# Setup and retention of an encoder trunk in one block: what is loaded, summed and turned first

## The chip, the cores and the metric

The kernel runs on one core of a Trainium2 chip. The metric is the device time of one execution, in microseconds. The core has five engines with queues of their own: TensorE (PE, with its weight loads as PEld), VectorE (DVE), ScalarE (ACT), GpSimd (POOL) and SyncE (SP), which here issues nearly all DMAs. They wait for each other by semaphores.

## The reference, cut to what matters

A trunk of two layers over 2048 tokens of width 1024. Each layer modulates its normalised input by a shift and a scale that a matrix product of `silu(c)` gives; the first layer then projects it for a retention and an attention part.

```
cos, sin = _rope_tables(positions)
c_act = silu(c)
mod = c_act @ ada_w[layer] + ada_b[layer]
shift, scale, gate = split(mod, (1024, 1024, 1024))
h = rmsnorm(x, pre_g[layer]) * (1 + scale) + shift
z = h @ w_in                      # even layer: rq, rk, rv, rg, ... are columns of z
rq, rk = rope(rq), rope(rk) * 64 ** -0.5
lg = log_sigmoid(dec)             # decay of each of 4 heads, two directions
o = retention forward + retention backward, chunks of 128 tokens
```

The change touches only the beginning: the loads, the modulation sums, the rotary angles, the decays, and the first of 16 tiles of the retention's projection.

## The kernel before, in words

The kernel is a sequence of blocks. Within a block each engine runs its own program; at the end of a block all engines meet and the block's semaphores are cleared. The first block is `setup`, the second `project_retention`; attention, the odd layer and the output follow and are not touched.

`setup` loads five small tensors (`cols`, `const`, `table`, `dec_row`, `pos_i`), two tiles of x (`xt`), eight blocks `ada` of 128 rows of the modulation matrix (128x2048, 1 MB each) and the retention's weights `w_raw` in three column groups of four pieces (512 KB each), all from SP's queue in the order of `L227` to `L246`. All engines that need a small load wait for all five (`small_in` at 80).

* VectorE computes `lg`, the log of a sigmoid, with some 25 operations on 128x8 elements, each waiting for the one before (`L354` to `L370`), then the angles' whole turns (`L388` to `L390`), the exponents (`L375` to `L377`), and then the modulation: two of the eight blocks go to TensorE as matrix-vector products (`mod_ps`, `L327`), six are multiplied by `silu_c` and added up in PSUM by VectorE (`acc_ps`, `L395`, `L398`). The last sum goes to SBUF (`mod_sums`), TensorE transposes it in 16 pieces (`L332`), VectorE reduces these four at a time (`L414`) and makes `shift` and `gain` (`L417` to `L421`).
* GpSimd reduces the angles (`ang`, `bit`, `red`, `L289` to `L309`): turns times a constant, subtracted, three times over, then clipped. ScalarE takes sine and cosine (`L273`).
* A weight is kept as two float32r parts, high and low: ScalarE rounds `w_raw` to `w_hi`, and VectorE or GpSimd subtracts, `w_lo = w_raw - w_hi`. The first column group is split in `setup` (`L271`, `L406`, `L311`), the others at the start of the next block (`split_w`, `L585`, `L640`, `L691`), two pieces of each group on GpSimd and two on VectorE.

`project_retention` runs over 16 tiles of 128 tokens, the last first. For a tile, TensorE transposes the scaled x (`ps_h`), ScalarE applies `gain` and `shift` (`ht`), h is split into `h_hi` and `h_lo`, and each of three projections (`ps_qk`, `ps_v`, `ps_g`) is 24 products, three for each of eight 128-row pieces. VectorE multiplies `ps_qk` by cosine and sine (`rc`, `rs`), GpSimd adds and weights them (`qk`, `qf`, `kw`, `L627` to `L633`), TensorE transposes them and forms the state's product (`ps_kv`, `L798`). For the first tile the halves of h go to ScalarE and VectorE (`L588`, `L695`), and TensorE waits for all four `w_lo` pieces of a group before `ps_v` and before `ps_g`. The second tile begins with its first `ps_qk` product (`L761`).

Of the kernel before, what the change touches and what calls it, by code (L numbers as in the profile page):

```python
# [19 lines left out]
P = 128  # L20
D = 1024
# [136 lines left out]
def setup(nc, st, const, cols, row, positions, turning, ada_w, layer, w, w_hi, w_lo, w_raw, w_in, xt, x_pieces, xn, ps_h, spare):  # L158


    with ExitStack() as ctx:
# [3 lines left out]
        sem = counters(nc, ctx)  # L165

        NW, NPE = 6, 2
        dec_row = sb("dec_row", [1, 2 * H])
        pos_i = sb("pos_i", [P, NT], I32)
        pos = sb("pos", [P, NT])  # L170
        ang, turns_i, turns, red, bit = turning
        low = sb("low", [P, 2 * H])
        mods = sb("mods", [P, 2 * KD])
        logit = sb("logit", [P, 2 * H])
        lg = st.lg
        tiny = sb("tiny", [P, 8, 2 * H])
        expw = sb("expw", [P, 2 * H])
        expq = sb("expq", [P, H, 2])
        expk = sb("expk", [P, H, 2])
        ada = sb("ada", [P, NW, 2 * D])  # L180
        acc = spare[:]
        scale1 = sb("scale1", [P, KD])
        mods_pe = sb("mods_pe", [P, 2 * KD])
        sq = xn[:]
        ssq, ms, rstd = [[sb(f"{n}_x{i}", [P, 1]) for i in range(2)] for n in ("ssq", "ms", "rstd")]
        dec_ps = ctx.enter_context(nc.psum_tensor("dec_ps", [P, BANK], F32))
        mod_ps = ctx.enter_context(nc.psum_tensor("mod_ps", [P, BANK], F32))
        acc_ps = ctx.enter_context(nc.psum_tensor("acc_ps", [P, 2 * D], F32))

        small_in = sem("small_in")  # L190
        x_ahead = [sem(f"x_ahead{i}") for i in range(2)]
        ada_in = [sem(f"ada_in{i}") for i in range(NW)]
        c_ready = sem("c_ready")
        mod_sum = sem("mod_sum")
        mod_turned = sem("mod_turned")
        mod_first = sem("mod_first")
        whi_done = sem("whi_done0")
        pos_ready = sem("pos_ready")
        ang_ready = sem("ang_ready")
        turn_ready = sem("turn_ready")  # L200
        bit_ready = sem("bit_ready")
        red_step = sem("red_step")
        dec_done = sem("dec_done")
        v_step = sem("v_step")
        e_ready = sem("e_ready")
        a_step = sem("a_step")
        sq_done = sem("sq_done")
        ms_done = sem("ms_done")
        rstd_done = sem("rstd_done")
        xn_done = sem("xn_done0")  # L210
        x0_turned = sem("x0_turned")
        w0_in = [sem(f"w0_in{k}") for k in range(KD // 2)]

        ident = st.const[:, C_ID:C_ID + P]
        ones = st.const[:, C_ONE:C_ONE + P]

        w_view = w.rearrange("(k a p) n -> k p a n", p=P, a=2)
        ada_view = ada_w.rearrange("(k p) n -> k p n", p=P)
        block = ctx.enter_context(nc.Block())

        def place(k):

            return k if k < NW else k - NW + NPE

        @block.sync
        def _(sp):
            sp.dma_start(st.cols[:], cols).then_inc(small_in, 16)  # L227
            sp.dma_start(st.const[:], const[:, 0:C_FWD]).then_inc(small_in, 16)
            sp.dma_start(st.table[:], const[:, C_FWD:C_END]).then_inc(small_in, 16)
            sp.dma_start(dec_row[:], row[:, R_DEC:R_END]).then_inc(small_in, 16)  # L230
            sp.dma_start(pos_i[:], positions).then_inc(small_in, 16)
            sp.dma_start(xt[:, 0, :], x_pieces[0]).then_inc(x_ahead[0], 16)
            def load_w(j, k, arrived):
                sp.dma_start(w_raw[:, 2 * k:2 * k + 2, j * BANK:(j + 1) * BANK],
                             w_view[k][:, :, j * BANK:(j + 1) * BANK]).then_inc(arrived, 16)

            for k in range(KD):
                if k == NW:
                    sp.dma_start(xt[:, 1, :], x_pieces[1]).then_inc(x_ahead[1], 16)
                if k >= NW:  # L240
                    sp.wait_ge(mod_sum, k - NW + 1)
                sp.dma_start(ada[:, place(k), :], ada_view[k][:, 0:2 * D]).then_inc(ada_in[place(k)], 16)
            for k in range(KD // 2):
                load_w(0, k, w0_in[k])
            for j in range(1, 3):
                for k in range(KD // 2):  # L246
                    load_w(j, k, w_in[j])

        @block.scalar
        def _(act):  # L250
            act.wait_ge(small_in, 80)
            act.activation(st.silu_c[:], st.cols[:, K_C:K_C + KD], ACT.Silu).then_inc(c_ready, 1)
            act.wait_ge(v_step, 3)
            act.activation(tiny[:, 1, :], tiny[:, 0, :], ACT.Exp, scale=-1.0).then_inc(a_step, 1)
            act.wait_ge(x_ahead[0], 16)
            act.activation(sq, xt[:, 0, :], ACT.Square, accum_out=ssq[0][:]).then_inc(sq_done, 1)
            act.wait_ge(rstd_done, 1)
            act.activation(xn[:], xt[:, 0, :], ACT.Copy, scale=rstd[0][:]).then_inc(xn_done, 1)
            act.wait_ge(e_ready, 1)
            act.activation(st.q_w[:], expq[:], ACT.Exp)  # L260
            act.activation(st.k_w[:], expk[:], ACT.Exp)
            act.activation(st.c_w[:].rearrange("p d h -> p (d h)"), expw[:], ACT.Exp).then_inc(a_step, 1)
            act.wait_ge(x_ahead[1], 16)
            act.wait_ge(x0_turned, 1)
            act.activation(sq, xt[:, 1, :], ACT.Square, accum_out=ssq[1][:]).then_inc(sq_done, 1)
            act.wait_ge(rstd_done, 2)
            act.activation(xn[:], xt[:, 1, :], ACT.Copy, scale=rstd[1][:])
            for k in range(KD // 2):
                at = slice(2 * k, 2 * k + 2), slice(0, BANK)
                act.wait_ge(w0_in[k], 16)  # L270
                act.activation(w_hi[:, *at], w_raw[:, *at], ACT.Copy).then_inc(whi_done, 1)  # L271
            act.wait_ge(red_step, 5)
            act.activation(st.sin[:].rearrange("p t f -> p (t f)"), red[:, 0, :], ACT.Sin)  # L273
            act.activation(st.cos[:].rearrange("p t f -> p (t f)"), red[:, 1, :], ACT.Sin)

        @block.gpsimd
        def _(pool):
            pool.memset(st.neg_half[:], -0.5).then_inc(ms_done, 1)
            def norm(i):
                pool.wait_ge(sq_done, i + 1)  # L280
                pool.tensor_scalar(ms[i][:], ssq[i][:], 1.0 / D, EPS, ALU.mult, ALU.add).then_inc(ms_done, 1)
                pool.wait_ge(ms_done, i + 2)
                pool.tensor_tensor(rstd[i][:], ms[i][:], st.neg_half[:, 0:1], ALU.pow).then_inc(rstd_done, 1)

            norm(0)

            pool.wait_ge(pos_ready, 1)
            freq = st.table[:, C_FREQ - C_FWD:C_FREQ - C_FWD + HALF]
            pool.tensor_tensor(ang[:], pos[:].unsqueeze(2).broadcast_to([P, NT, HALF]),  # L289
                               freq.unsqueeze(1).broadcast_to([P, NT, HALF]), ALU.mult).then_inc(ang_ready, 1)  # L290
            angf = ang[:].rearrange("p t f -> p (t f)")
            pool.wait_ge(ang_ready, 1)
            pool.wait_ge(turn_ready, 1)
            pool.tensor_scalar(bit[:], turns[:], -6.28125, None, ALU.mult).then_inc(bit_ready, 1)
            pool.wait_ge(bit_ready, 1)
# [2799 lines left out]
```

## Time and profile before

| | us |
|---|---|
| median of 3 runs (2311.18 to 2315.13) | 2313.79 |
| the profiled execution, its own time | 2312.47 |
| its span, first to last instruction | 2310.6 |
| TensorE busy in the span | 2242.0 (97%) |
| VectorE, ScalarE, GpSimd busy | 1370.0, 1125.9, 900.6 |

Busy shares are means over stages with different limits. For this change the first 66 us count. There, a row of the timeline tells when an instruction started and how long it took; what stands in brackets behind it is the idle time of its engine before it and what ended that.

### The profile page before, as it was taken

Reading aid. Unit: us, or ns where it says so; the run is one execution under the profiler, and the core shown is the slowest. Engines: PE = TensorE matmul, PEld = TensorE weight load, DVE = VectorE, ACT = ScalarE, POOL = GpSimd, SP = SyncE. Lnnn points to the kernel's source line nnn. Section 1 sums busy time; section 2 is a strip of 40 time slices with the busy share of each in tenths; the row PEclk is TensorE's granted clock in tenths of the full one; section 3 lists DMA queues with packets and bytes.
Section 4 is the critical chain, followed back from the end, with each engine's and each line's share of the span. In section 5 each row is a group of like instructions: output and inputs, shape, how many; then the busy total and the mean of one; then the engine's idle time right before and its main releaser. Section 6 shows DMA issues by size and latency. Waiting matters only on the chain. (4 is left out here: it accounts for less than half of the span.)

```text
span 2310.6 us, 31013 instructions
## 1 busy us (share of the span) xinstructions
PE 2242.0 (97%) x11298; PEld 1884.8 (82%) x11298; DVE 1370.0 (59%) x2083; ACT 1125.9 (49%) x2095; POOL 900.6 (39%) x665
## 2 busy tenths in 40 slices
PE   5999999999999999999999989998999999999998
PEld 5888888898897788888888878887888888888886
DVE  7333336343435776767677642115999999994442
ACT  5555534222224555555555535556555566663432
POOL 6322222232222111101101023232999999992454
PEclk9999999999999999999999999999999999999999
DMA  7533323534444222222131323331111211145553
GB/s 304 183 136 136 136 78 132 173 120 151 137 149 141 56 65 69 65 69 65 32 83 33 105 105 112 134 118 37 46 55 42 69 55 42 64 167 163 157 172 101
DMA packets 151298, 245.75 MB, mean 106 GB/s; under 512 B 8964, under 2 KB 95236, under 8 KB 146566
## 3 DMA queue, kind: packets, MB, share of 16 engines
q1 hardware_dynamic: 146566, 235.73, 31.0%
q10 hardware_dynamic: 4608, 8.39, 1.0%
q8 instruction: 75, 1.23, 0.2%
q14 instruction: 49, 0.40, 0.1%
HBM read 157.84 MB, written 86.25 MB: 106 GB/s over the span
## 5 line engine op out<-in xcount | busy, mean ns | idle before, releaser
L2410 POOL TENSOR_TENSOR conv_g<-conv_g,product 128x1024 f32<-128x1024 f32 x160 | 385.0, 2408 | 34.2 <-ACT product L2459 24.5
L2554 DVE SCALAR_TENSOR_TENSOR ps_b<-u,cols,ps_b 128x1024 f32<-128x1024 f32 x304 | 391.7, 1288 | 9.2
L2670 PE MATMUL ps_a<-ho_hi,wp_lo 128*128 128x512 f32 x768 | 300.2, 391 | 6.8 <-DVE h_left L2610 6.8
L2671 PE MATMUL ps_a<-h_left,wp_hi 128*128 128x512 f32 x768 | 299.6, 390 | 0.0
L2672 PE MATMUL ps_a<-ho_hi,wp_hi 128*128 128x512 f32 x768 | 299.5, 390 | 0.0
L2459 ACT ACTIVATE product<-u,cols 128x1024 f32<-128x1024 f32 x160 | 183.3, 1151 | 170.3 <-POOL conv_g L2410 169.0
L1771 DVE TENSOR_TENSOR pt_lo<-ps_pt,pt_hi 128x512 fp32r<-128x512 f32 x256 | 176.1, 688 | 136.0 <-ACT pt_hi L1666 134.0
L1666 ACT ACTIVATE pt_hi<-ps_pt 128x512 fp32r<-128x512 f32 x256 | 154.4, 604 | 202.9 <-PE ps_pt L1858 202.1
L1761 DVE TENSOR_REDUCE mx<-ps_s 128x1 f32<-128x512 f32 x248 | 168.2, 683 | 34.3 <-PE ps_s L1850 32.6
L1659 ACT ACTIVATE probs<-ps_s,bias 128x512 f32<-128x512 f32 x248 | 168.8, 700 | 17.6 <-DVE bias L1767 9.3
L2670 PEld LDWEIGHTS ps_a<-ho_hi,wp_lo 128*128 128x128 f32 x768 | 144.6, 188 | 38.6 <-DVE h_left L2610 8.7
L2672 PEld LDWEIGHTS ps_a<-ho_hi,wp_hi 128*128 128x128 f32 x768 | 144.6, 188 | 30.1
L2671 PEld LDWEIGHTS ps_a<-h_left,wp_hi 128*128 128x128 f32 x768 | 144.4, 188 | 29.8
L1721 POOL TENSOR_TENSOR q_lo<-q_st,q_hi 128x512 fp32r<-128x512 f32 x15 | 26.9, 1793 | 342.6 <-DVE q_hi L1754 342.6
L1858 PEld LDWEIGHTS ps_pt<-const,probs 128*128 128x128 f32 x1024 | 127.0, 140 | 38.1 <-DVE pt_lo L1771 4.7
L1858 PE MATMUL ps_pt<-const,probs 128*128 128x128 f32 x1024 | 154.0, 273 | 2.1 <-DVE pt_lo L1771 2.1
L1846 PE MATMUL ps_s<-k_hi,q_lo 128*128 128x512 f32 x248 | 111.0, 448 | 7.6 <-ACT probs L1659 5.0
L1867 PE MATMUL ps_ot<-pt_hi,v_lo 128*128 128x512 f32 x256 | 111.9, 437 | 0.3 <-DVE pt_lo L1771 0.3
L2924 PE MATMUL ps_a<-w_last_hi,mo_lo 128*128 128x512 f32 x256 | 101.1, 395 | 1.8 <-PEq L2200 1.7
L1869 PE MATMUL ps_ot<-pt_hi,v_hi 128*128 128x512 f32 x256 | 100.7, 393 | 0.0
L1868 PE MATMUL ps_ot<-pt_lo,v_hi 128*128 128x512 f32 x256 | 100.2, 391 | 0.0
L2926 PE MATMUL ps_a<-w_last_hi,mo_hi 128*128 128x512 f32 x256 | 99.9, 390 | 0.0
(445 smaller groups left out, 5435.4 us busy)
## 6 DMA issues: line engine op xcount, KB each, us to landing
scratch_ret_pack<-pack SPq DMA_DIRECT2D x14, 1280.0 KB, 5.5
pack<-scratch_ret_pack SPq DMA_DIRECT2D x14, 1280.0 KB, 6.4
ada<-in_ada_w_dram SPq DMA_DIRECT2D x16, 768.0 KB, 6.1
wp_raw<-in_od_w_in_dram SPq DMA_DIRECT2D x24, 512.0 KB, 3.9
xt<-in_x_dram SPq DMA_DIRECT2D x16, 512.0 KB, 6.2
ada<-in_ada_w_dram SPq DMA_DIRECT2D x8, 1024.0 KB, 9.3
mix_e<-scratch_mix SPq DMA_DIRECT2D x16, 512.0 KB, 4.5
x_e<-in_x_dram SPq DMA_DIRECT2D x16, 512.0 KB, 5.0
```

The lines of the kernel that those rows point to most:

```text
L1659: act.activation(probs[s][b][:, kb * BANK:(kb + 1) * BANK], bank_of(n, b, kb), ACT.Exp, bias=bias[b % 2][:], scale=SCALE, accum_out=sums[s ...
L1666: act.activation(pt_hi[kt % 4][:], ps_pt[kt % 2][:], ACT.Copy).then_inc(pthi_done, 1)
L1761: dve.tensor_reduce(mx[:, kb:kb + 1], bank_of(n, b, kb), AX.X, ALU.max).then_inc(max_done, 1)
L1771: dve.tensor_tensor(pt_lo[kt % 4][:], ps_pt[kt % 2][:], pt_hi[kt % 4][:].bitcast(F32), ALU.subtract).then_inc(ptlo_done, 1)
L1858: mm = pe.transpose(ps_pt[kt % 2][:, qb * P:(qb + 1) * P], probs[sl][qb][:, kt * P:(kt + 1) * P], ident)
L1867: pe.matmul(ps_o[sl][:], v_lo[:, kt, :], pt_hi[kt % 4][:], start=kt == 0, stop=False)
L2410: pool.tensor_tensor(half(conv_g, h), half(conv_g, h), product[adds(c, i, h) % 2][:], ALU.add).then_inc(added, 1)
L2459: act.activation(product[adds(c, i, h) % 2][:], units(c, V_TAPS + i, h), ACT.Copy, scale=tap_w).then_inc(product_done, 1)
L2554: dve.scalar_tensor_tensor(acc[h], units(c, k, h), params(c, k), acc[h], ALU.mult, ALU.add).then_inc(tap, 1)
L2670: pe.matmul(dst, lo[:, k, :], h_hi[:, k, t], start=k == 0, stop=False)
L2671: pe.matmul(dst, hi[:, k, :], h_lo[:, k, t], start=False, stop=False)
L2672: mm = pe.matmul(dst, hi[:, k, :], h_hi[:, k, t], start=False, stop=k == KD - 1)
```

## The change

`setup` is no longer a block. Its instructions are put at the head of each engine's program in `project_retention`, and the meeting of the engines between the two goes; what needs `gain` waits for a semaphore, `gain_ready`.

* SP's queue begins with the first x tile and the eight modulation blocks; blocks 7 and 8 come in halves. The second x tile comes after the first group of weights. The five small loads go to ScalarE's queue.
* VectorE turns the angles before the polynomial of `lg`, and the polynomial has one operation per coefficient where it had two. Blocks 7 and 8 are summed in halves, and TensorE transposes the first half while the second is summed.
* The three products of the angle reduction (`bit0`, `bit1`, `bit0` again) go from GpSimd to ScalarE.
* The first group's weights are split piece by piece: two `w_hi` before `gain`, two behind the first tile's `h_hi`; two `w_lo` each on GpSimd and VectorE. The second x tile is squared and scaled in this stage, between the `w_hi` pieces. The halves of `w_lo` change hands: GpSimd has pieces 0 and 1 of the first group and 2 and 3 of the others, VectorE the rest. TensorE waits for each piece of `w_lo` before the products that read it.

```diff
+        sp.dma_start(xt[:, 0, :], x_pieces[0]).then_inc(x_ahead[0], 16)
+        for k in range(late):
+            sp.dma_start(ada[:, k, :], ada_view[k][:, 0:2 * D]).then_inc(ada_in[k], 16)
+        for k in range(late, KD):
+            sp.wait_ge(mod_sum, k - late + 1)
+            for a in range(2):
+                half = slice(a * D, (a + 1) * D)
+                sp.dma_start(ada[:, slot(k), half], ada_view[k][:, half]).then_inc(half_in[2 * (k - late) + a], 16)
+        for k in range(KD // 2):
+            load_w(0, k, w0_in[k])
+        sp.dma_start(xt[:, 1, :], x_pieces[1]).then_inc(x_ahead[1], 16)
...
+        act.dma_start(st.cols[:], cols).then_inc(small_in, 16)
+        act.dma_start(su.dec_row[:], row[:, R_DEC:R_END]).then_inc(small_in, 16)
+        act.dma_start(su.pos_i[:], positions).then_inc(small_in, 16)
+        act.dma_start(st.table[:], const[:, C_FWD:C_END]).then_inc(small_in, 16)
+        act.dma_start(st.const[:], const[:, 0:C_FWD]).then_inc(small_in, 16)
+        act.wait_ge(small_in, 80)
+        act.activation(st.silu_c[:], st.cols[:, K_C:K_C + KD], ACT.Silu).then_inc(c_ready, 1)
...
+        act.wait_ge(turn_ready, 1)
+        act.activation(bit0[:], turns[:], ACT.Copy, scale=-6.28125).then_inc(bit_ready, 1)
+        act.activation(bit1[:], turns[:], ACT.Copy, scale=-0.0019350051879882812).then_inc(bit_ready, 1)
+        act.wait_ge(rstd_ready, 1)
+        act.activation(xn[:], xt[:, 0, :], ACT.Copy, scale=rstd[:, 0:1]).then_inc(xn_ready, 1)
+        act.wait_ge(e_ready, 1)
+        act.activation(st.q_w[:], expq[:], ACT.Exp)
+        act.activation(st.k_w[:], expk[:], ACT.Exp)
+        act.activation(st.c_w[:].rearrange("p d h -> p (d h)"), expw[:], ACT.Exp).then_inc(a_step, 1)
+        act.wait_ge(red_step, 2)
+        act.activation(bit0[:], turns[:], ACT.Copy, scale=-3.0199159819e-07).then_inc(bit_ready, 1)
...
+        for a in range(2):
+            pool.tensor_tensor(red[:, a, :], bit0[:, a, :], angf, ALU.add).then_inc(red_step, 1)
+        for i, bit in enumerate((bit1, bit0)):
+            pool.wait_ge(bit_ready, 2 + i)
+            pool.wait_ge(red_step, 2 + i)
+            pool.tensor_tensor(red[:], red[:], bit[:], ALU.add).then_inc(red_step, 1)
...
+        for a in range(2):
+            pe.wait_ge(mod_sum, KD - 1 + a)
+            for m in range(a * KD, (a + 1) * KD):
                 mm = pe.transpose(acc_ps[:, m * P:(m + 1) * P], acc[:, m * P:(m + 1) * P], ident)
...
-            act.sem_inc(ss_ready, 2)
-            act.sem_inc(xn_ready, 2)
-            def split_w(j):
-                act.wait_ge(w_in[j], 64)
-                for k in range(KD // 2):
-                    at = slice(2 * k, 2 * k + 2), slice(j * BANK, (j + 1) * BANK)
-                    act.activation(w_hi[:, *at], w_raw[:, *at], ACT.Copy).then_inc(whi_done, 1)
-
...
+            su.scalar(act)
+            first_hi(0)
+            first_hi(1)
+            act.wait_ge(gain_ready, 1)
...
-            split_w(1)
-            split_w(2)
+            first_hi(2)
+            first_hi(3)
+            act.wait_ge(x_ahead[1], 16)
+            act.wait_ge(h_turned, 1)
+            act.activation(xn[:], xt[:, 1, :], ACT.Square, accum_out=ssq[:, 1:2]).then_inc(ss_ready, 1)
+            split_w(1, 0)
+            act.wait_ge(rstd_ready, 2)
+            act.activation(xn[:], xt[:, 1, :], ACT.Copy, scale=rstd[:, 1:2]).then_inc(xn_ready, 1)
+            for k in range(1, KD // 2):
+                split_w(1, k)
+            for k in range(KD // 2):
+                split_w(2, k)
...
-            split_w(1)
-            split_w(2)
+            su.gpsimd(pool)
+            split_w(0, 0)
+            split_w(0, 1)
+            rstds(pool, 1, 1)
+            for j in range(1, 3):
+                for k in range(2, 4):
+                    split_w(j, k)
...
+            split_w(0, 2)
+            split_w(0, 3)
+            su.fold(dve)
             dve.memset(back[:], 0.0).then_inc(back_copied, 1)
             dve.wait_ge(back_copied, 1)
-            split_w(1)
-            split_w(2)
+            for j in range(1, 3):
+                for k in range(2):
+                    split_w(j, k)
+            dve.wait_ge(turned_angles, 1)
```

What stood at the head of SP's queue, the queue of SyncE's DMAs, before:

```order
L227 DMA cols<-in_columns_dram 128x373
L228 DMA const<-in_consts_dram 128x256
L229 DMA table<-in_consts_dram 128x292
L230 DMA dec_row<-in_rows_dram 1x8
L231 DMA pos_i<-in_positions_dram 128x16
L232 DMA xt<-in_x_dram 128x1024
L242 DMA ada<-in_ada_w_dram 128x2048 x6
L239 DMA xt<-in_x_dram 128x1024
L242 DMA ada<-in_ada_w_dram 128x2048 x2
L234 DMA w_raw<-in_ev_w_in_dram 128x2x512 x12
```

and what stands there now:

```order
L231 DMA xt<-in_x_dram 128x1024
L233 DMA ada<-in_ada_w_dram 128x2048 x6
L238 DMA ada<-in_ada_w_dram 128x1024 x4
L228 DMA w_raw<-in_ev_w_in_dram 128x2x512 x4
L241 DMA xt<-in_x_dram 128x1024
L228 DMA w_raw<-in_ev_w_in_dram 128x2x512 x8
```

The five small loads have gone to ScalarE's queue; the second x tile has moved behind four weight pieces.

On VectorE, between the small loads and the modulation sums (`acc_ps`), `tiny` holding the polynomial's values, there now stands:

```order
L334 TENSOR_SCALAR low<-logit 128x8
L337 TENSOR_SCALAR turns_i<-ang 128x512
L338 TENSOR_SCALAR turns_i<-ang 128x512
L339 CAST turns<-turns_i 128x1024
L342 TENSOR_SCALAR tiny<-tiny 128x8
L343 RECIPROCAL tiny<-tiny 128x8
L344 TENSOR_TENSOR tiny<-tiny 128x8
L345 TENSOR_TENSOR tiny<-tiny 128x8
L346 TENSOR_SCALAR tiny<-tiny 128x8
L348 SCALAR_TENSOR_TENSOR tiny<-tiny 128x8 x7
L349 SCALAR_TENSOR_TENSOR tiny<-tiny 128x8
L350 TENSOR_TENSOR lg<-low,tiny 128x8
```

Before, `turns_i` and `turns` stood behind `lg`; now the polynomial, `lg` and the exponents stand behind `turns`.

On ScalarE, behind the first tile's h (`ht`, `h_hi`), before:

```order
L588 ACTIVATE ht<-ps_h,shift,gain 128x128 x4
L592 ACTIVATE h_hi<-ht 128x512
L594 ACTIVATE h_hi<-ht 128x512
L585 ACTIVATE w_hi<-w_raw 128x2x512 x8
L559 ACTIVATE ht<-ps_h,shift,gain 128x128 x8
```

and now:

```order
L577 ACTIVATE ht<-ps_h,shift,gain 128x128 x4
L581 ACTIVATE h_hi<-ht 128x512
L583 ACTIVATE h_hi<-ht 128x512
L565 ACTIVATE w_hi<-w_raw 128x2x512 x2
L588 ACTIVATE xn,ssq<-xt 128x1024
L570 ACTIVATE w_hi<-w_raw 128x2x512
L591 ACTIVATE xn<-xt,rstd 128x1024
L570 ACTIVATE w_hi<-w_raw 128x2x512 x7
L542 ACTIVATE ht<-ps_h,shift,gain 128x128 x8
```

Two `w_hi` of the first group (`L565`) and the two passes over the second x tile have come between `h_hi` and the eight `w_hi` of the other groups.

## Rows read from the trace of the kernel before

**Rows 1.** The page, its first line.

```profile
span 2310.6 us, 31013 instructions
```

**Rows 2.** Windows: length, busy time (instructions) of PE, PEld, DVE, ACT, POOL; clock, DMA share, GB/s.

```profile
10.00:20.00 10.00, 9.49 (x45) 9.49 (x46) 9.34 (x19) 0.86 (x4) 6.29 (x5) 1.00 1.01 426
40.00:50.00 10.00, 6.24 (x19) 5.02 (x20) 6.68 (x9) 9.15 (x13) 5.47 (x2) 0.61 0.68 256
150.00:250.00 100.00, 100.00 (x504) 84.36 (x503) 35.03 (x52) 52.04 (x94) 27.31 (x34) 1.00 0.40 139
```

**Rows 3.** TensorE's waits, 40 to 260 us: us in total, times, longest.

```profile
PE ps_qk L761 <- DVE h_lo L699: 9.6, 1, 9.6
```

**Rows 4.** Timeline 2 to 25 us: start, duration, instruction.

```profile
2.50 0.35 SPq L231 DMA_DIRECT2D pos_i<-in_positions_dram  x1
5.33 0.21 ACT L252 ACTIVATE silu_c<-cols 128x8 f32<-128x8 f32 x1 [3.32 <-DMA pos_i<-in_positions_dram]
9.24 1.06 POOL L289 TENSOR_TENSOR ang<-pos,table 128x512 f32<-128x512 f32 x1
9.43 0.89 DVE L366 TENSOR_TENSOR tiny<-tiny 128x8 f32<-128x8 f32 x1
12.19 0.43 DVE L388 TENSOR_SCALAR turns_i<-ang 128x512 int32<-128x512 f32 x1
12.98 0.69 DVE L390 CAST turns<-turns_i 128x1024 f32<-128x1024 int32 x1
14.83 2.34 DVE L395 TENSOR_SCALAR acc_ps<-ada,silu_c 128x2048 f32<-128x2048 f32 x1
16.73 2.50 POOL L297 TENSOR_TENSOR red<-bit,ang 128x512 f32<-128x512 f32 x2
22.16 2.37 POOL L302 TENSOR_TENSOR red<-red,bit 128x1024 f32<-128x1024 f32 x1
```

**Rows 5.** Timeline 25 to 39 us.

```profile
25.59 2.36 DVE L398 SCALAR_TENSOR_TENSOR acc_ps<-ada,silu_c,acc_ps 128x2048 f32<-128x2048 f32 x1 [1.03 <-DMA ada<-in_ada_w_dram]
30.45 3.68 PE L332 MATMUL acc_ps<-const,mod_sums 128*128 128x128 f32 x16 [4.52 <-DVE mod_sums L398]
34.56 2.48 DVE L414 TENSOR_REDUCE mods<-acc_ps 128x4 f32<-128x512 f32 x4
35.75 2.34 POOL L311 TENSOR_TENSOR w_lo<-w_raw,w_hi 128x1024 fp32r<-128x1024 f32 x1
37.08 1.05 DVE L417 TENSOR_TENSOR mods<-mods,mods_pe 128x16 f32<-128x16 f32 x1
38.44 0.17 DVE L421 SCALAR_TENSOR_TENSOR gain<-scale,cols 128x8 f32<-128x8 f32 x1
```

**Rows 6.** Timeline 40 to 58 us: ScalarE, GpSimd, VectorE.

```profile
40.81 1.51 ACT L588 ACTIVATE ht<-ps_h,shift,gain 128x128 f32<-128x128 f32 x4 [3.84 <-PEq L101]
43.41 7.68 ACT L585 ACTIVATE w_hi<-w_raw 128x1024 fp32r<-128x1024 f32 x8
44.52 12.43 POOL L640 TENSOR_TENSOR w_lo<-w_raw,w_hi 128x1024 fp32r<-128x1024 f32 x4 [6.43 <-ACT w_hi L585]
46.46 11.57 DVE L691 TENSOR_TENSOR w_lo<-w_raw,w_hi 128x1024 fp32r<-128x1024 f32 x4 [1.61 <-ACT w_hi L585]
```

**Rows 7.** Timeline 59 to 66 us: GpSimd's rotation, TensorE's second tile.

```profile
59.31 0.91 POOL L627 TENSOR_TENSOR qk<-rc,rs 128x256 f32<-128x256 f32 x1 [2.36 <-DVE rs L671]
63.05 1.04 POOL L633 TENSOR_TENSOR kw<-qk,k_w 128x512 f32<-128x512 f32 x1
65.42 0.48 PE L761 MATMUL ps_qk<-w_hi,h_lo 128*128 128x512 f32 x1
```

**Rows 8.** SP's eight loads from 2063.8 us; ScalarE's DMAs: 25 before, four beside.

```profile
w_last<-in_od_w_out_dram SPq DMA_DIRECT2D x8, 512.0 KB, 9.2
...
DMA to landing us min/median/max: 2.4/2.4/5.5
...
DMA to landing us min/median/max: 5.5/6.9/7.6
```

More of the change, by code:

```diff
@@ L161, in setup, with project_retention @@
+def project_retention(nc, st, su, sums, const, cols, row, positions, w, x_pieces, x, xt, xn, ps_h, w_hi, w_lo, w_raw, h_hi, h_lo,
+                      pack, ahead, ada_w):
     with ExitStack() as ctx:
@@ L165, in setup @@
         sem = counters(nc, ctx)
[L167 to L179, printed above, removed]
@@ L203, in setup @@
[L203 to L217, printed above, removed]
@@ L218, in setup @@
[L218 to L242, printed above, removed]
-            for k in range(KD // 2):
[L244 to L247, printed above, removed]
@@ L427, in project_retention @@
-def project_retention(nc, st, x, xt, xn, ps_h, w_hi, w_lo, w_raw, w_in, h_hi, h_lo, pack, ahead, ada_w):
-    with ExitStack() as ctx:
-        def sb(name, shape, dt=F32):
-            return ctx.enter_context(nc.sbuf_tensor(name, shape, dt))
-        sem = counters(nc, ctx)
-        ssq = sb("ssq", [P, 2])
-        ms = sb("ms", [P, 2])
-        rstd = sb("rstd", [P, 2])
+        ssq, ms, rstd = sums
         ht = sb("ht", [P, 2, KD, P])
@@ L2994, in hybrid_trunk @@
         x_pieces = [x[(NT - 1 - i) * P:(NT - i) * P, :] for i in range(2)]
-        w_in = [weights.enter_context(nc.semaphore(f"w1_in{j}")) for j in range(3)]
         half = NT * HALF
@@ L3002, in hybrid_trunk @@
                    in_packs("turns", 3 * half, [P, 2, half]), in_packs("red", 5 * half, [P, 2, half]),
-                   in_packs("bit", 7 * half, [P, 2, half]))
-        setup(nc, st, consts, columns, rows, positions, turning, ada_w[0], 0, ev_w_in, w_hi, w_lo, w_raw, w_in, xt, x_pieces, xn, ps_h, spare)
+                   in_packs("bit0", 7 * half, [P, 2, half]), in_packs("bit1", half, [P, 2, half]))
+        sums = [weights.enter_context(nc.sbuf_tensor(n, [P, 2], F32)) for n in ("ssq", "ms", "rstd")]
+        su = setup_room(nc, turning, spare, xn)
         lora = QR + KVR
@@ L3010, in hybrid_trunk @@
         ahead = [(first_raw[:, k:k + 4, :], first_view[:, k:k + 4, RET_COLS:RET_COLS + lora]) for k in (0, 4)]
-        project_retention(nc, st, x, xt, xn, ps_h, w_hi, w_lo, w_raw, w_in, h_hi, h_lo, pack, ahead, ada_w[0])
+        project_retention(nc, st, su, sums, consts, columns, rows, positions, ev_w_in, x_pieces, x, xt, xn, ps_h, w_hi, w_lo, w_raw,
+                          h_hi, h_lo, pack, ahead, ada_w[0])
         weights.close()
```

437 lines of the change are left out of this document (226 added, 211 removed).

## The prediction

> **What bounds the kernel now.** I began with the span and the windows. The profiled execution spans 2310.6 us [rows 1], its own time is 2312.47 us, and the median of the three runs is 2313.79 us, 1.3 us above it. In the last window, inside the retention stage, TensorE is busy 100.00 of 100 us [rows 2], so an earlier start of that stage should arrive at the end one for one. I then asked what TensorE waits for between 40 and 260 us: one long wait, 9.6 us for the first low part of h [rows 3]. So the change can only be worth what it moves on the chain that ends in that wait and in the first tile behind it. I read that chain as a timeline from the start [rows 4, 5] up to the moment at which TensorE begins the second tile, 65.42 us [rows 7]; from there on it has no long wait. That moment is my yardstick. The reader should see four marks: the small loads are usable at 5.33 us (`silu_c` starts), the modulation sums start at 14.83 us [rows 4], `gain` ends at 38.61 us [rows 5], the second tile starts at 65.42 us.
>
> A second thing has to be seen, because it decides the sum. A tiny vector operation takes 0.17 us [rows 5], but 0.89 us when it is issued into a GpSimd operation: `L366` issued at 9.43 us ends at 10.32, just after `ang` (9.24 to 10.30) [rows 4]. `mods` issued at 37.08 us ends at 38.13, just after GpSimd's `w_lo` (35.75 to 38.09) [rows 5]. And where both engines have four `w_lo` subtractions ready, all eight take from 44.52 to 58.03 us, 13.5 us, or 3.38 us for one of each [rows 6]; GpSimd alone needs 2.34 us for one [rows 5], so VectorE's 1.0 us is simply added. The two engines take turns. The large modulation sums on VectorE, whose second input is in PSUM, are not held up: 2.36 us beside a busy GpSimd [rows 5]. The Trainium skill (SBUF — State Buffer, section "SBUF: two separate sides") gives the reason: a port pair that VectorE, for operations with two SBUF inputs, and GpSimd hold exclusively for a whole instruction. The trace agrees; by the rule alone the sum would be the same.
>
> **The change, step by step.** All times are from the arrival T of the small loads, then added up.
>
> *Arrival T, 5.33 us before.* The five small loads move from the head of SP's queue to ScalarE's queue, and x and six 1 MB blocks are put in SP's queue at the same moment. Before, the fifth small load was issued at 2.50 us and usable 2.8 us later [rows 4]. ScalarE issues five as fast, so the last goes out at about 2.5 us. The bound from below is that the two queues don't touch: T = 5.3. What the trace shows of the other case is `odd_gate`, the only DMA on ScalarE's queue: 2.4 us to landing as a rule, but 5.5 to 7.6 us (median 6.9) for the four that were issued while SP's queue held eight 512 KB loads [rows 8]. A load issued at 2.5 us with 6.9 us, less 0.3 us because the last one is half as large, lands at 9.1. The bound from above: x and the four blocks issued ahead of the last small load (0.5 + 4 x 1.05 MB) go first; at 426 GB/s, the rate of the window from 10 us [rows 2], that is 11.1 us from the first issues at about 1 us, with the completion T = 13. I take 9.1, the nearest row: **+3.8 us**.
>
> *T to the first sum, 9.5 us before (5.33 to 14.83).* The polynomial is shorter: 14 operations where there were 21, 1.4 us saved at 0.2 us each. But it now comes after the angle turns, in the very time when GpSimd runs its angle additions. `ang` and three small operations behind it end at T + 2.0; the two `turns_i` and `turns` (0.43, 0.4 and 0.69 us) at T + 3.5 [rows 4]. ScalarE's first product (about 1.0 us, as a `w_hi` pass, [rows 6]) releases GpSimd at T + 4.6; until then VectorE has done five or six of the 14. Then GpSimd runs two additions (2.50 us together) and one of 2.37 us [rows 4], and VectorE gets one tiny operation between each. At T + 9.9 GpSimd must wait, since ScalarE's third product is queued behind the exponents that VectorE is still to deliver. The remaining nine operations take 1.6 us: the sums start at T + 11.5. If the tiny operations were not held up, it would be T + 7.3. I take the lock as rows 4 show it: **+2.0 us**.
>
> *The sums, 15.6 us before (14.83 to 30.40, 1.03 of it a wait for the seventh block, [rows 5]).* Four whole ones at 2.36 us and a hand-over of 0.06, four halves at half of that: 14.6 us. Blocks 7 and 8 no longer wait behind the second x tile, and VectorE starts late enough that none is waited for: **-1.0 us**.
>
> *Last sum to `gain`, 8.2 us before (30.40 to 38.61).* Sixteen transposes took 3.68 us; now the first eight start a half sum earlier, and the last eight end 2.4 us after the last sum. One reduction of 0.62 us (four took 2.48) and four small operations, 0.7 us, follow; the two `w_lo` that stood before the reductions are now behind h, and `mods` has no GpSimd operation to wait out unless GpSimd's second `w_lo` is in flight then (up to 2.3 us, kept for the range). 3.9 us: **-4.3 us**. So `gain` ends at 9.1 + 11.5 + 14.6 + 3.9 = 39.1 us, against 38.61: the early gain is spent.
>
> *`gain` to the second tile, 26.8 us before (38.61 to 65.42).* The block boundary goes: `ht` started at 40.81 us on ScalarE, 2.2 us after `gain` [rows 5, 6]. Against it stands what was done before `gain` and now comes behind it on ScalarE: two `w_hi` of the first weights, the square and the scaling of the second x tile. ScalarE's queue after `gain`: `ht` 1.5 us, `h_hi` 1.0, then seven passes of 0.96 us [rows 6] (two first `w_hi`, square, one `w_hi`, scaling, two `w_hi`), with hand-overs 10.0 us. Only then may GpSimd begin its four `w_lo` of the second and third weights; before, it began at 44.52 us, 5.9 us after `gain`. From there VectorE and GpSimd take turns: 4 x 2.34 for GpSimd, 2 x 1.04 and one gate operation of 0.5 for VectorE, 11.9 us. `h_lo` of the second tile, 1.0 us, comes next, then GpSimd's rotation: 59.31 to 64.09 us, 4.8 us less the turn of `h_lo` inside it, 3.7 us, and TensorE's products of the state, 1.0 us [rows 7]. Together 27.7 us: **+0.9 us**. TensorE itself is not the limit there: its last six products wait for GpSimd's last `w_lo` and end about 1.4 us behind it, some 2 us before the rotation delivers. Waiting for `w_lo` in pieces lets it begin earlier and wait later.
>
> Sum: 3.8 + 2.0 - 1.0 - 4.3 + 0.9 = +1.4 us. On the profiled 2312.47 us this is 2313.9 us; on the median, **2315.2 us**. The weights' arrival is not on this path: they are asked for after the last block as before, and ScalarE reaches them later than they land. The three products that ScalarE takes over from GpSimd are hidden behind the sums before and after.
>
> **The rivals.** *Small loads on time* (T = 5.3). For it: ScalarE's queue is empty at that moment, and its loads are small. Against it: rows 8. The sum falls by 3.8 us to -2.4: 2311.4 us, no measurable change.
>
> *Faster: on time, and the tiny operations slip through.* For it: GpSimd's spans are rough, and a tiny operation needs 0.17 us. Against it: rows 4 and 5. The sums then start when the third block lands, about 14.2 us, which takes 2.6 us more off: -5.0 us, 2308.8 us.
>
> *Slower: each small load waits its turn behind a large one.* The mechanism is the mix of two queues on the same DMA engines, its price 1 us of end for 1 us of T, and it decides against the change from T = 12.3 on. At T = 13 the sum is +5.3 us, 2319.1 us. For it: all five small loads are waited for together, and a single one was late by up to 5.2 us behind such a queue [rows 8]. The Trainium skill (DMA: Bandwidth & Descriptors, section "Queues, rings and completion order") says that a DMA engine goes round the queues packet by packet, a packet being some 9 to 17 descriptors; its section "Issuing engines are not separate DMA queues" adds that issuing from several engines saves only issue time. By that rule the fifth small load waits for about four large shares, which is this rival; rows 8 bear it out in part.
>
> A smaller price could come on top of each. Between 40 and 50 us the granted clock was 0.61 of full, the lower level, 1.2 GHz, in part of it, behind a long idle time; 19 products took 6.24 us there, against 504 in 100 us later [rows 2]. Should the clock fall again in the 2 us before the rotation delivers, about 2 us are lost.
>
> **How the numbers follow.** The forecast (T from 7.5 to 11.5, lock as in the rows) holds 0.45 and spans -0.2 to +3.8 us; small loads on time 0.2; the fast rival 0.17; the slow one 0.18. What a measurement of this kernel can tell from no change is about 0.2%, 4.6 us: the first two lie within it, the fast rival just outside, the slow one outside for the most part. So faster 0.18, same 0.65, slower 0.17. The range, 2308.4 to 2320.0 us, goes from the fast rival to the slow one with half a microsecond for the spread of runs.
>
> **What would show it.** In the changed profile: `silu_c` near 9 us (5.3: on time; 12 or more: the slow rival). Vector operations of the polynomial of over 0.5 us beside `red` (the lock). The first sum 11.5 us after `silu_c`. `gain` near 39 us. GpSimd's `w_lo` of the second and third weights starting some 10 us after `gain` and then taking turns with VectorE. The second tile's first product near 66.8 us. I am wrong if `gain` ends by 34 us, or if the rotation starts much less than 23 us after `gain`; or if the time between the second tile and the end is not the same in both.

## The result, and the profile after

The changed kernel takes 2321.36 us (median of 7 runs, 2316.05 to 2322.65) against 2311.76 us (7 runs of the kernel before): ratio 1.0044, 95% interval 1.0034 to 1.0053. It is slower by about 10 us; forecast was +1.4 us, and 2320.0 us was the upper end of the range. The profiled execution took 2322.51 us; the first line of its page answers to [rows 1]:

```profile
span 2320.6 us, 30987 instructions
```

The timeline of the changed kernel, 15 to 72 us, at the marks of the prediction, answers to [rows 4 to 7]:

```profile
15.48 0.21 ACT L253 ACTIVATE silu_c<-cols 128x8 f32<-128x8 f32 x1 [10.66 <-DMA const<-in_consts_dram]
19.70 5.47 DVE L348 SCALAR_TENSOR_TENSOR tiny<-tiny 128x8 f32<-128x8 f32 x7
...
25.85 2.35 DVE L361 TENSOR_SCALAR acc_ps<-ada,silu_c 128x2048 f32<-128x2048 f32 x1
38.10 2.46 DVE L371 SCALAR_TENSOR_TENSOR mod_sums<-ada,silu_c,acc_ps 128x1024 f32<-128x1024 f32 x2
43.86 0.18 DVE L380 TENSOR_TENSOR mods<-mods,mods_pe 128x16 f32<-128x16 f32 x1
44.35 0.17 DVE L384 SCALAR_TENSOR_TENSOR gain<-scale,cols 128x8 f32<-128x8 f32 x1
...
47.49 0.80 PE L771 MATMUL ps_qk<-w_hi,h_lo 128*128 128x512 f32 x1 [4.40 <-DVE h_lo L701]
54.45 11.72 POOL L635 TENSOR_TENSOR w_lo<-w_raw,w_hi 128x1024 fp32r<-128x1024 f32 x4 [3.16 <-ACT w_hi L570]
56.30 5.07 DVE L691 TENSOR_TENSOR w_lo<-w_raw,w_hi 128x1024 fp32r<-128x1024 f32 x2 [1.61 <-ACT w_hi L570]
66.13 1.72 POOL L620 TENSOR_TENSOR qk<-rc,rs 128x256 f32<-128x256 f32 x1
69.89 0.66 PE L795 MATMUL ps_qf<-const,qf 128*128 128x128 f32 x4 [2.01 <-POOL qf L623]
71.81 0.48 PE L771 MATMUL ps_qk<-w_hi,h_lo 128*128 128x512 f32 x1
```

The reader should see the first row: ScalarE waits 10.66 us for the small loads, and `silu_c` starts at 15.48 us, where it started at 5.33 [rows 4] and 9.1 was forecast. Behind it the marks keep the distances that were forecast, to within 1.1 us. The steps, before and after:

| step | forecast | measured |
|---|---|---|
| T, `silu_c` starts | 9.1 us, +3.8 | 15.48 us, **+10.2** |
| T to first sum (25.85) | 11.5 us, +2.0 | 10.4 us, +0.9 |
| the sums (to 40.56) | 14.6 us, -1.0 | 14.7 us, -0.9 |
| last sum to `gain` (ends 44.52) | 3.9 us, -4.3 | 4.0 us, -4.2 |
| `gain` to second tile (71.81) | 27.7 us, +0.9 | 27.3 us, +0.5 |
| second tile, all of these | +1.4 | +6.4 |
| the span's end | +1.4 | +10.0 |

What stood in the queues in that time is told by the DMA view of the changed kernel, three stretches in turn: 6 to 8, 8 to 10 and 0 to 14.4 us (q1 is SP's queue, q10 ScalarE's; packets, MB, share of the engines):

```profile
q1 hardware_dynamic: 117, 0.83, 99.1%
q10 hardware_dynamic: 113, 0.01, 3.8%
...
q1 hardware_dynamic: 105, 0.73, 86.7%
q10 hardware_dynamic: 105, 0.10, 15.0%
...
q1 hardware_dynamic: 679, 4.51, 78.0%
q10 hardware_dynamic: 575, 0.48, 10.6%
```

A packet of this view is about one row of a load: in e7 below, x and three blocks, 512 rows, count as 576, 16 more for each load. Packets of the two queues go in about equal numbers, though one of SP's carries 6 to 8 KB on average and one of ScalarE's 1 KB or less. From 6 to 8 us 113 packets bring 0.01 MB: these are the 64-byte rows of `pos_i`. From 4 to 6 us the counts are not equal, 116 of SP's to 64; why, no run shows.

### The profile page after: what moved, and what is told of

It reads as the page before. It is cut to its first block and busy times, and to the rows that moved or that the text cites. A ratio compares the mean times of both kernels' runs of the same rounds, so it can differ in the third digit from the quotient of the medians.

```text
span 2320.6 us, 30987 instructions
## 1 busy us (share of the span) xinstructions
PE 2243.9 (97%) x11298; PEld 1885.7 (81%) x11298; DVE 1371.1 (59%) x2077; ACT 1128.0 (49%) x2098; POOL 892.5 (38%) x663
## 5 line engine op out<-in xcount | busy, mean ns | idle before, releaser
L2931 PE MATMUL ps_a<-w_last_lo,mo_hi 128*128 128x512 f32 x256 | 100.3, 392 | 0.0
```

## The experiments

T is the start of `silu_c`, "second tile" the first product behind the state's; both from the profiled execution, us. Each run was timed beside the kernel before on the same chip (medians 2310.4 to 2311.2 us).

| run | T | second tile | time, runs | ratio to before |
|---|---|---|---|---|
| before | 5.33 | 65.42 | | |
| changed | 15.48 | 71.81 | 2321.36, 7 | 1.0044 |
| b1 small loads on ACT | 13.87 | 74.45 | 2320.91, 4 | 1.0046 [1.0031, 1.0061] |
| e1 small loads at head | 5.07 | 64.75 | 2309.66, 11 | 0.9994 [0.9985, 1.0003] |
| e2 large loads wait | 5.86 | 63.14 | 2312.54, 10 | 1.0007 [0.9997, 1.0016] |
| e3 e1, polynomial first | 4.67 | 63.10 | 2307.72, 11 | 0.9988 [0.9979, 0.9997] |
| e4 e1, `w_lo` on VectorE | 4.67 | 60.85 | 2304.46, 10 | 0.9974 [0.9965, 0.9983] |
| e5 e1, second x early | 5.19 | 63.30 | 2310.15, 11 | 0.9992 [0.9983, 1.0001] |
| e6 e3 + e4 + e5 | 4.96 | 60.91 | 2305.29, 12 | 0.9979 [0.9971, 0.9988] |
| e7 wait after three blocks | 13.32 | 70.52 | 2317.12, 6 | 1.0028 [1.0016, 1.0041] |
| e8 `pos_i` at head | 13.19 | 69.84 | 2316.23, 10 | 1.0021 [1.0012, 1.0031] |
| e9 blocks in halves | 11.02 | 67.61 | 2312.57, 10 | 1.0011 [1.0002, 1.0021] |
| e10 e3 + e4 | 4.67 | 59.31 | 2303.85, 9 | 0.9969 [0.9958, 0.9979] |
| b2 before, `w_lo` on VectorE | 4.77 | 65.14 | 2307.49, 11 | 0.9987 [0.9978, 0.9996] |

### Is it the small loads? b1, e1, e2

Theory A: the place of the five small loads makes the whole loss, since everything waits for them. Rival B: joining the blocks and the new order cost it. b1 does only this part of the change to the kernel before; e1 takes it out of the changed kernel; e2 leaves the loads where the change puts them and lets the large ones wait. One of the five moved lines stands for all.

```diff
 b1 (before)
-            sp.dma_start(st.cols[:], cols).then_inc(small_in, 16)
+            act.dma_start(st.cols[:], cols).then_inc(small_in, 16)
 e1 (changed)
-        act.dma_start(st.cols[:], cols).then_inc(small_in, 16)
+        sp.dma_start(st.cols[:], cols).then_inc(small_in, 16)
         sp.dma_start(xt[:, 0, :], x_pieces[0]).then_inc(x_ahead[0], 16)
 e2 (changed)
         sp.dma_start(xt[:, 0, :], x_pieces[0]).then_inc(x_ahead[0], 16)
+        sp.wait_ge(small_in, 80)
```

> The kernel before with one edit: the five small loads are issued from ScalarE's queue instead of the head of SP's. Theory A (the small loads land only behind the large loads that SP issues at the same time, and all else follows): silu_c starts near 15 us instead of 5.3, gain ends near 48.5 us, the time rises by 9 to 10 us, about 2321. Theory B (the loss comes from joining the blocks and from what was reordered in them, the queue does not matter): silu_c within 1 us of 5.3, time within 2 us of before.

> The changed kernel with the five small loads back at the head of SP's queue. Theory A: silu_c near 5.4 us, the first modulation sum near 15.8, gain near 34.5, the second tile near 61.8 us, time 10 us below the changed kernel, about 2311.5, no more than 0.1% from before. Theory B: silu_c comes early too, but the time stays at 2318 or more.

> The changed kernel, small loads still on ScalarE's queue, but SP issues the first modulation block only when they have all landed. Theory A (the mixing with SP's large loads is the cause): silu_c near 5.5 us, blocks start some 4 us later than in the changed kernel, first sum near 16 us, time 2311 to 2314. A rival within A (ScalarE's queue is slow by itself): silu_c after 8 us. Theory B: time stays at 2318 or more.

b1 alone loses what the change loses (1.0046 against 1.0044); e1 and e2 are within 0.1% of the kernel before. A holds, B falls: joined and reordered, but with the loads in time, the block costs nothing and gains nothing that can be measured. One mark missed its expectation: e1's second tile came at 64.75 us, not at 61.8, for two reasons that stand below, `gain` 1.5 us later than expected and a lower TensorE clock.

### How do they come late? e7, e8, e9

e7 makes the queue in front of SP's loads shorter, and its expectation was worked out by interpolation:

```diff
         for k in range(late):
+            if k == 3:
+                sp.wait_ge(small_in, 80)
```

> The changed kernel with the small loads on ACT's queue as it has them, and SP waiting for them after three of its six whole blocks. Theory A (the small loads land only behind what SP has queued by then): silu_c begins when x and three blocks are in, half-way between 5.9 (x alone queued) and 15.5 (x and six), at 9 to 11 us, and the first sum 10.4 us after that, at 19 to 22; the time, by the marks, 2314 to 2318. Rival (ACT's queue is slow by itself once SP's is deep, whatever the depth): silu_c still begins at 14 to 16 us, or at 5 to 7 if three blocks are too few to matter.

T was 13.32, in neither range. Up to 12 us its queues look like those of the changed kernel (477 small packets through, there 472); then SP's three blocks are through, and the other 101 packets go in a single microsecond. DMA view of e7, 12 to 13 us:

```profile
q10 hardware_dynamic: 101, 0.09, 25.7%
q1 hardware_dynamic: 25, 0.07, 18.7%
```

So the small loads are not slow by themselves, and 477 of their packets went while SP's blocks did. That led to theory P: the queues take turns packet by packet, and a small load costs its number of packets. Two edits tell it from a share by bytes. e8 takes only `pos_i`, 8 KB, out of ScalarE's queue; e9 leaves all five there and makes SP's packets half as large (VectorE's wait for a block changes as TensorE's does):

```diff
 e8
-        act.dma_start(su.pos_i[:], positions).then_inc(small_in, 16)
+        sp.dma_start(su.pos_i[:], positions).then_inc(small_in, 16)
         sp.dma_start(xt[:, 0, :], x_pieces[0]).then_inc(x_ahead[0], 16)
 e9
-            sp.dma_start(ada[:, k, :], ada_view[k][:, 0:2 * D]).then_inc(ada_in[k], 16)
+            for a in range(2):
+                half = slice(a * D, (a + 1) * D)
+                sp.dma_start(ada[:, k, half], ada_view[k][:, half]).then_inc(ada_in[k], 16)
...
-            pe.wait_ge(ada_in[k], 16)
+            pe.wait_ge(ada_in[k], 32)
```

> The changed kernel with one of the five small loads, pos_i (8 KB), taken from ACT's queue to the head of SP's. Theory P (the two queues take turns packet by packet, so that what a small load costs is its number of packets and not its bytes): in the changed kernel's trace ACT's queue moved 113 packets with 0.01 MB between 6 and 8 us, beside 117 of SP's, which is pos_i; without those turns silu_c begins some 2 us earlier, at 13.0 to 13.8 us instead of 15.48, and the time is 2318 to 2320. Rival B (the queues share by bytes, or ACT's queue waits for the large loads as wholes): 8 of 479 KB change nothing, silu_c at 15.2 to 15.6 and the time that of the changed kernel, 2321.

> The changed kernel with each of the first six modulation blocks loaded as two halves, 4 KB instead of 8 KB in a row, and the small loads left on ACT's queue. Theory P (turns packet by packet): a turn of SP's queue is half as long; 578 small packets beside 578 of 4.1 KB are 2.85 MB, 6.8 us at the 0.42 MB/us of the full queues, so that from 2.2 us on they are through at about 9 to 9.5, silu_c begins at 9.5 to 11 us, and the time falls by 4.5 to 6 to 2315.5 to 2317. Rival B (bytes or whole transfers): silu_c stays at 15 to 16 and the time at 2321.

The timeline of e8, one row:

```profile
13.19 0.21 ACT L253 ACTIVATE silu_c<-cols 128x8 f32<-128x8 f32 x1 [9.30 <-DMA const<-in_consts_dram]
```

The timeline of e9, one row:

```profile
11.02 0.21 ACT L255 ACTIVATE silu_c<-cols 128x8 f32<-128x8 f32 x1 [6.27 <-DMA const<-in_consts_dram]
```

And the DMA view of e9, 8 to 10 and 0 to 10.4 us:

```profile
q1 hardware_dynamic: 170, 0.63, 80.3%
q10 hardware_dynamic: 169, 0.16, 23.7%
...
q1 hardware_dynamic: 743, 2.73, 68.1%
q10 hardware_dynamic: 578, 0.48, 14.1%
```

In T both are as P has them (e9 at the upper edge). 8 KB less on ScalarE's queue took 2.3 us off T, and halves, without touching the small loads, 4.5 us: still one packet for one, but 169 in the 2 us in which there were 105, and 2.73 MB of SP's went ahead instead of 4.51. The difference, 1.78 MB, is 4.2 us at the 0.42 MB/us of the full queues. The times fell too, each taken against the kernel before beside it, by 3.8 and 7.4 us, more than T, and so lie below what was expected.

One rival is not settled by T: that a small load waits, as a whole, for all that SP issued before it. Both edits change that as well, since in e8 the last small load was issued 0.9 us earlier, and in e9 SP had issued about four half blocks by then instead of four whole ones. What decides against it are the counts. Alone, ScalarE's queue moved 422 packets in 1 us (e2); a load that waited as a whole would then go in one burst. But 113 packets of `pos_i` took 2 us, and even in stretches of half a us the counts are equal: 40 to 40, 25 to 24 and 26 to 26 from 6.5 to 8 us in the changed kernel.

### What the block could gain: e3, e4, e5, e6, e10, b2

e3 is e1 with the three angle operations on VectorE (`turns_i` twice, `turns`) moved behind the polynomial, whose small operations then don't meet GpSimd's `red`.

> As e1_small_at_head, and VectorE computes the polynomial before the angle turns, as in the kernel before, so that it does not run beside GpSimd's angle additions. If the two engines take turns for tiny operations: polynomial operations 0.17 to 0.2 us each, no group of 5 us, first sum when the third block lands, 14 to 14.5 us instead of 15.8, gain 1.5 to 2.5 us earlier than in e1, time 1.5 to 2.5 us below e1. If the turns do not matter: no change to e1 or up to 1 us slower, since the angles start later.

Timeline of e1:

```profile
9.29 5.49 DVE L348 SCALAR_TENSOR_TENSOR tiny<-tiny 128x8 f32<-128x8 f32 x7
15.87 2.35 DVE L361 TENSOR_SCALAR acc_ps<-ada,silu_c 128x2048 f32<-128x2048 f32 x1 [0.33 <-DMA ada<-in_ada_w_dram]
33.89 1.67 DVE L380 TENSOR_TENSOR mods<-mods,mods_pe 128x16 f32<-128x16 f32 x1
...
35.87 0.17 DVE L384 SCALAR_TENSOR_TENSOR gain<-scale,cols 128x8 f32<-128x8 f32 x1
45.98 11.73 POOL L635 TENSOR_TENSOR w_lo<-w_raw,w_hi 128x1024 fp32r<-128x1024 f32 x4 [3.17 <-ACT w_hi L570]
61.42 1.12 PE L795 MATMUL ps_qf<-const,qf 128*128 128x128 f32 x4 [2.01 <-POOL qf L623]
63.19 1.84 PE L804 MATMUL ps_kv<-pack,kw 128*128 128x128 f32 x8
64.75 0.50 PE L771 MATMUL ps_qk<-w_hi,h_lo 128*128 128x512 f32 x1
```

Timeline of e3:

```profile
7.60 1.38 DVE L343 SCALAR_TENSOR_TENSOR tiny<-tiny 128x8 f32<-128x8 f32 x7
14.95 2.35 DVE L361 TENSOR_SCALAR acc_ps<-ada,silu_c 128x2048 f32<-128x2048 f32 x1 [3.81 <-DMA ada<-in_ada_w_dram]
```

The seven operations take 1.38 us instead of 5.49, and the second tile comes 1.65 us earlier, but the one is not shown to make the other. In e1, too, the sums waited for the third block in the end, for 0.33 us; in e3 that block itself came 0.92 us earlier, with the same loads in the same order, and `gain` with it. Had it come to e1 as early, the polynomial would have held the sums up by 0.6 us, and that is what its order could be worth there. The other 0.75 us of the second tile is TensorE's lower clock, which set in earlier in e1. The times of e1 and e3 have overlapping intervals.

e4 is e1 with the low halves of `w` of the second and third group on VectorE alone; b2 does the same to the kernel before. The edit of e4 (TensorE's waits for these pieces go by VectorE's semaphore):

```diff
 GpSimd
-            for j in range(1, 3):
-                for k in range(2, 4):
-                    split_w(j, k)
 VectorE
             for j in range(1, 3):
-                for k in range(2):
+                for k in range(KD // 2):
                     split_w(j, k)
```

> The changed kernel with its small loads at the head of SP's queue, and with the low halves of w of the second and third group on VectorE alone; GpSimd keeps two of the first group. Theory C (behind the gain GpSimd's turns bound the block: its four low halves took 11.73 us, its rotation is queued behind them, and TensorE waits 2.0 us for that, then runs at the lower clock): GpSimd is free for the rotation as soon as qk stands, the low halves on VectorE take 1.2 us each, the wait before ps_qf and the stretch at 0.50 go, and the second tile begins 2 to 4 us earlier than with the small loads at the head alone (at 61 to 63 us against 64.75); the time follows to 2306 to 2308. Rival D (ScalarE's high halves bound it, whoever takes the low ones): the second tile begins within 1 us of 64.75 and the time stays at 2309 to 2311.

> The kernel before with nothing changed but the low halves of w: all eight of the second and third group on VectorE, none on GpSimd. Theory C (two engines that take turns are no faster than one alone): VectorE does the eight at about 1.2 us each behind ScalarE's high halves, done by 54 to 55.5 us instead of 58.0; the rotation and the second tile come 2.5 to 4 us earlier, second tile at 61.5 to 63, time 2307 to 2309. Rival (the second tile waits for something else, or VectorE alone is slower than the two): second tile at 65 to 67 and no gain, 2311 or more.

Timeline of e4:

```profile
8.89 1.37 DVE L348 SCALAR_TENSOR_TENSOR tiny<-tiny 128x8 f32<-128x8 f32 x7
15.90 2.35 DVE L361 TENSOR_SCALAR acc_ps<-ada,silu_c 128x2048 f32<-128x2048 f32 x1 [2.70 <-DMA ada<-in_ada_w_dram]
...
35.84 0.17 DVE L384 SCALAR_TENSOR_TENSOR gain<-scale,cols 128x8 f32<-128x8 f32 x1
38.99 0.79 PE L768 MATMUL ps_qk<-w_hi,h_lo 128*128 128x512 f32 x1 [5.83 <-DVE h_lo L698]
44.94 8.04 DVE L688 TENSOR_TENSOR w_lo<-w_raw,w_hi 128x1024 fp32r<-128x1024 f32 x7 [1.00 <-ACT w_hi L570]
54.25 0.92 POOL L620 TENSOR_TENSOR qk<-rc,rs 128x256 f32<-128x256 f32 x1 [11.47 <-DVE rs L666]
60.85 0.48 PE L768 MATMUL ps_qk<-w_hi,h_lo 128*128 128x512 f32 x1
```

Windows of e1 and e4, 60 to 62 and 62 to 64 us (columns as in [rows 2]); first e1:

```profile
60.00:62.00 2.00, 0.57 (x3) 0.58 (x4) 0.00 (x0) 0.00 (x0) 1.92 (x3) 0.85 0.00 0
62.00:64.00 2.00, 2.00 (x11) 2.00 (x10) 0.00 (x0) 0.68 (x1) 1.11 (x3) 0.50 0.00 0
```

and e4:

```profile
60.00:62.00 2.00, 2.00 (x15) 1.83 (x14) 0.84 (x2) 1.98 (x2) 0.00 (x0) 1.00 0.02 4
62.00:64.00 2.00, 2.00 (x11) 1.64 (x10) 1.01 (x4) 1.99 (x4) 0.00 (x0) 1.00 0.03 8
```

VectorE alone does one piece in 1.15 us; GpSimd, with VectorE in turn, did four in 11.73 us. GpSimd's rotation starts at 54.25 us instead of 57.68, TensorE never waits for it, and its clock stays up. The second tile comes 3.9 us and the end 5.2 us earlier than in e1, both better than expected. e4 beats both kernels. Its first two rows bear on e3: here the polynomial has e1's order, but `red` began only at 10.66 us, behind the seven operations, which took 1.37 us; the sums began at 15.90 all the same, when the third block had landed.

In b2 the low halves were done early too, and the rotation came at 55.27 us instead of 59.31, but the second tile only 0.3 us earlier: TensorE has no wait there between its first product (43.70) and the second tile (65.14). In the kernel before it waits 0.5 us in that stretch, so it is itself the bound, and my expected 61.5 to 63 was wrong. The time fell by 2.9 us all the same; why, these marks don't show.

e5 is e1 with the second x tile loaded ahead of blocks 7 and 8, and squared and scaled before `gain`, so that ScalarE has only `w_hi` behind h. e6 joins e3, e4 and e5; e10 leaves e5 out.

> The changed kernel with its small loads at the head, the second x tile loaded ahead of the last two modulation blocks, and its square and scaling done before the gain stands. Rival D (ScalarE's order behind the gain bounds the block): its high halves begin some 2 to 4 us earlier, the second tile begins at 61 to 63 us against 64.75, and the time is 2306 to 2308. Theory C (GpSimd's turns bound it): GpSimd gets its high halves earlier but takes as long, so the rotation begins earlier by no more than the 2 us by which the first of them comes earlier; and if the x tile's 0.5 MB holds up the last two blocks, the gain is 1 to 2 us later, second tile 64 to 66, time 2309 to 2312.

> The small loads at the head of SP's queue, the polynomial ahead of the angles on VectorE, the low halves of the second and third group on VectorE alone, and the second x tile early. If the parts add up, from 64.75 for the second tile with the loads at the head alone: polynomial first -1.6, low halves on VectorE -2 to -4, x early 0 to -3; second tile at 57 to 61 us and a time of 2301 to 2306, faster than both kernels by 0.2 to 0.4%. If one bound hides the others, it is no better than the best of the parts, 2306 to 2308.

> The small loads at the head of SP's queue, the polynomial ahead of the angles, and the low halves of the second and third group on VectorE alone; the second x tile where the changed kernel has it. If the two edits add up: second tile at 60.85 - 1.65 = 59.2 us and a time of 2302 to 2304. If the low halves alone set the block's end (they come as ScalarE delivers the high ones): second tile at 60 to 61, 2304 to 2305.5.

e5 moved the second tile by 1.45 us, to 63.30, between the two ranges that were expected, and the time not measurably: GpSimd began its four `w_lo` 3.4 us earlier (42.59 us), but VectorE's four took 10.65 us in turn with them, and `gain` was 0.9 us later. With VectorE alone there is nothing left for e5 to give: e6 is no better than the best of its parts, e4, though its time lies in the wide range that was given for a sum of the parts. e3 and e4 add up in the mark (59.31, expected 59.2), but 1.0 of the 1.5 us is again the third block, which let the sums begin at 14.87 us in e10. e10, 2303.85 us, 0.31% below the kernel before, is the best here, though e4 is within its interval.

## Why the prediction was wrong

**T, the step that failed.** The prediction took 9.1 us for T, "the nearest row", [rows 8]; it was 15.48. That row is one transfer on ScalarE's queue, late by 4.5 us (6.9 against 2.4) behind eight of SP's. It was not a load but a store of 256 KB to a DRAM tensor, `odd_gate`, and the last of the four was issued at 2081.8 us, when the eight loads had landed. The kernel before, DMA view from 2064 to 2076 us, and the four by their line:

```profile
scratch_odd_gate<-gate ACTq DMA_DIRECT2D x2, 256.0 KB, 7.1
...
L2477 ACTq DMA_DIRECT2D scratch_odd_gate<-gate x4: 338/338/338, 2065.8 to 2081.8; - x4
```

Above all, the prediction took the delay of one transfer for the delay of five that follow each other in one queue, four of them with 128 rows to bring in turn. (The last was also issued at 3.0 us, not 2.5.) The slow rival came nearest: the two queues do hold each other up, and its price, T = 13, was 2.5 us short. But it counted x and the four blocks that had been issued ahead, 4.7 MB, 11.1 us; that 4.51 MB (10.7 us at 0.42 MB/us) did go ahead is luck, since that amount follows from the number of small rows and the size of a large one: with halves it was 2.73 MB. The rival left out the small loads' own 0.48 MB (1.1 us), and the queues started to flow at about 2 us instead of 1; 0.8 us stays unaccounted for. It had a chance of 0.18.

The Trainium skill (DMA: Bandwidth & Descriptors, section "Queues, rings and completion order") has the rule that a DMA engine goes round the queues packet by packet. The trace agrees: 105 packets to 105, whatever they carry, but for the stretch from 4 to 6 us. The page also gives some 9 to 17 descriptors to a packet; whether a turn here is one row or several, equal counts over all engines can't tell.

**T to the first sum.** Right in kind. The seven multiply-adds took 5.47 us beside GpSimd's `red` (1.38 without it, in e3), 10.4 us in all against 11.5. The rule of the Trainium skill that the prediction named (SBUF — State Buffer, "SBUF: two separate sides") agrees with 5.49 against 1.38 us, the same operations in e1 and e3.

**The sums, and last sum to `gain`.** Right to 0.1 us each. The caveat there, GpSimd's `w_lo` in front of `mods`, did not come true in the changed kernel (`mods` 0.18 us), but in e1, where `w_lo` is at 30.87 to 35.53 us: `mods` took 1.67 us, and `gain` ended 5.5 us after the last sum instead of 4.0. Loads in time brought that collision back.

**`gain` to the second tile.** 27.3 us against 27.7; GpSimd began its four `w_lo` 9.9 us after `gain` (10.0 forecast), and TensorE waited 2.0 us for the rotation, as forecast. The other small price, a lower clock behind that wait, is absent in the changed kernel, e2, e8 and e9 and stands in e1, e3 and e7: in e1 it is 0.50 of full, the 1.2 GHz level, from 62 to 64 us, where the state's products took 1.84 us, against 1.06 in e4. So h behind the sums did bring the first product closer to `gain` (3.0 us, where it was 5.2 in the kernel before), and this was given back in front of the rotation; e4, which takes the wait away, is 24.8 us from `gain` to the second tile.

**From there one for one.** Wrong by up to 4 us either way. The changed kernel's second tile is 6.4 us late, the last `ps_g` product of the retention stage 6.7, the first product that the next attention writes to `ps_ot` 9.6, the end 10.0. Of the 2.9 us between the second and the third of these, 2.6 are waits of TensorE in work that the change doesn't touch (`wi_lo` 0.7 us more, `heads_t` 1.3, `rot` 0.5, `wi_lo` of `ps_ckv` 0.1). In the 14 profiles that stretch takes from 394.6 us (e6) to 403.0 (e5), with no relation to an edit that I could find, but with one to TensorE's granted clock. Windows of that stretch (columns as in [rows 2]), first e6, then e5:

```profile
343.80:738.40 394.60, 381.60 (x2216) 339.47 (x2216) 184.71 (x499) 121.07 (x281) 102.74 (x133) 0.99 0.41 142
346.90:749.90 403.00, 388.82 (x2217) 344.74 (x2217) 187.95 (x499) 121.15 (x281) 101.96 (x133) 0.97 0.40 140
```

For the same products TensorE is busy 7.2 us longer in e5, at a mean clock of 0.97 against 0.99; the two profiles at 0.97 (e5, e2) are the longest there, 400.7 us and more, and the six at 0.99 take 394.6 to 397.5. A profile is one execution, and executions of one kernel spread as widely: e5's eleven runs take 2305.66 to 2314.43 us, and the profiled one is its slowest, e6's profiled one its fastest. Whether each kernel has its own mean there besides stays open. The later stages also decide the other cases in which mark and time part: e2 (2.3 us ahead of the kernel before at the mark, and no faster), b2, and the changed kernel against b1 (2.6 us ahead, and no faster).

## What to carry to other kernels

When small loads that everything waits for share the DMA engines with large ones on another queue, count rows, not bytes: here as many rows of the large ones went ahead as the small loads had, so 64-byte rows cost about as much as 1 KB rows. Put them ahead in the same queue, or let the large loads wait for them; a second issuing engine doesn't bring them sooner. And before splitting elementwise work between VectorE and GpSimd, look whether their durations in the trace just add: here VectorE alone was faster, and left GpSimd free for what TensorE waits for.

## What was not expected of the hardware

One load of 8 KB (128 rows of 64 bytes) cost 2.3 us of the start (e8), nearly as much as 1 MB of SP's loads at 0.42 MB/us. In e2, with SP's queue empty behind x, 422 small packets went in 1 us; in the changed kernel 575 took until 14.4 us. And the same wait of 2.0 us left TensorE's clock at 1.00 in the changed kernel, e2, e8 and e9, but was followed by 0.50 in e1, e3 and e7; what made the difference is open.
